# Where the low weights of one kind of unit lie in their slots: a 64-byte shift in a float32 split-matmul kernel

## What is computed

```python
# first block (cut)
zin = rmsnorm(x, gain) @ w_in                       # 2048 x 10240
q, k, v, g_attn, u, g_pool, m_attn, m_pool = split(zin)
y_attn = (stick_breaking_attention(q, k, v) * silu(g_attn)) @ w_attn_up
y_pool = (pooled(u) @ pool_w * pool_scale * silu(g_pool)) @ w_pool_up
x = x + (sigmoid(m_attn) * y_attn + sigmoid(m_pool) * y_pool) @ w_out
# second block (cut)
x = x + hybrid_mixer(rms_norm(x), ...)              # retention and gated delta rule, w_in_2, w_out_2
x = x + cross_attention(rms_norm(x), mem, w_xq_2, w_xkv_2, w_xo_2)
x = x + square(relu(rms_norm(x) @ w_ff1_2)) @ w_ff2_2
return rms_norm(x)
```

## Time and profile before

| | |
|---|---|
| median of three runs | 2882.5 us (2881.85 to 2883.88) |
| time of the profiled execution | 2884.14 us |
| its span, first to last instruction | 2882.4 us |
| TensorE busy | 2847.8 us, 99% |
| VectorE busy | 1931.6 us, 67% |
| ScalarE busy | 1354.6 us, 47% |
| mean DMA rate | 176 GB/s |

### The profile page before, as it was taken

The page is one execution under the profiler, slowest core; times in us unless marked ns, Lnnn a source line. Parts: engine busy times, 40 slices in busy tenths (PEclk is TensorE's granted clock), DMA queues, the critical chain, the costliest instruction groups (busy, mean ns, idle before and its releaser), DMA issues.

```text
span 2882.4 us, 38752 instructions
## 1 busy us (share of the span) xinstructions
PE 2847.8 (99%) x15872; PEld 2443.7 (85%) x15872; DVE 1931.6 (67%) x2513; ACT 1354.6 (47%) x1729; POOL 57.1 (2%) x102
## 2 busy tenths in 40 slices
PE   9999999999999999999999999999999999999998
PEld 8899888888888888888888888888888888888887
DVE  7645557678665658888888875456666555656556
ACT  5434654357443445555554543444345434444434
POOL 0000210000000000000000000000000000000000
PEclk9999999999999999999999999999999999999999
DMA  7544445564555544433333345544354445554453
GB/s 277 183 182 161 146 161 191 189 236 172 196 180 196 198 151 160 147 136 143 144 134 136 140 163 201 193 180 157 133 204 176 188 191 192 190 202 176 187 193 146
DMA packets 72849, 506.66 MB, mean 176 GB/s; under 512 B 8384, under 2 KB 8512, under 8 KB 12896
## 3 DMA queue, kind: packets, MB, share of 16 engines
q1 hardware_dynamic: 71136, 497.83, 46.8%
q0 software_dynamic: 1104, 5.90, 0.6%
q10 hardware_dynamic: 432, 0.45, 0.0%
HBM read 499.95 MB, written 2.10 MB: 174 GB/s over the span
## 4 chain that ended last, share of the span: by engine, by line
PE 86%; DVE 9%; ACT 3%; issue 2%; DMA 1%; SPq 0%; DVEq 0%; POOL 0%; ACTq 0%
PE double L1333 80%; PE bank L1333 5%; DVE cacc L2036 2%; DVE wlo L2030 2%; ACT whi L1692 1%; DVE cst L2053 1%; PE bank L1336 1%; DVE cacc L2033 1%; ACT L1888 0%; DVE Tn L2544 0%; DVE cst L2030 0%; DVE Cm L2030 0%; ACT tmp L1893 0%; DMA vec<-in_vec 0%; DMA raw<-in_wall 0%
## 5 line engine op out<-in xcount | busy, mean ns | idle before, releaser
L1333 PE MATMUL double<-AA,whi 128*128 128x512 f32 (+1 forms) x5008 | 1660.7, 383 | 3.5 <-DVE wlo L2030 3.5
L1333 PE MATMUL double<-AA,wlo 128*128 128x256 f32 (+1 forms) x4624 | 1302.1, 282 | 0.0
L1692 ACT ACTIVATE whi<-raw 128x1024 fp32r<-128x1024 f32 x926 | 925.0, 1049 | 790.1 <-PE double L1333 762.1
L2030 DVE TENSOR_TENSOR wlo<-raw,whi 128x1024 fp32r<-128x1024 f32 (+1 forms) x934 | 1101.4, 1214 | 233.2 <-ACT whi L1692 230.7
L1333 PEld LDWEIGHTS double<-AA,whi 128*128 128x128 f32 x5008 | 916.0, 188 | 197.5 <-DVE wlo L2030 5.1
L1333 PEld LDWEIGHTS double<-AA,wlo 128*128 128x128 f32 x4624 | 871.6, 188 | 1.5
L1333 PE MATMUL double<-whi,AA 128*128 128x512 f32 x1536 | 487.9, 393 | 0.5 <-DVE wlo L2030 0.5
L1333 PEld LDWEIGHTS double<-whi,AA 128*128 128x128 f32 x1536 | 288.4, 188 | 60.9 <-DVE wlo L2030 1.3
L1333 PE MATMUL double<-whi,BB 128*128 128x512 f32 x1024 | 316.9, 389 | 0.0
L1333 PE MATMUL double<-wlo,AA 128*128 128x512 f32 x768 | 299.0, 389 | 0.0
L1333 PEld LDWEIGHTS double<-whi,BB 128*128 128x128 f32 x1024 | 192.2, 188 | 40.3
(11 more groups left out here) (335 smaller groups left out, 1722.6 us busy)
## 6 DMA issues: line engine op xcount, KB each, us to landing
raw<-in_wall SPq DMA_DIRECT2D x462, 1024.0 KB, 4.9
raw<-in_wall SPq DMA_DIRECT2D x9, 256.0 KB, 6.6
X<-in_xT SPq DMA_DIRECT2D x1, 2048.0 KB, 11.4
Mm<-in_memT POOLq DMA_DIRECT2D x1, 2048.0 KB, 16.2
tmp<-rqk POOLq DMA_DIRECT2D x16, 128.0 KB, 2.2
mblk<-in_memT SPq DMA_DIRECT2D x8, 256.0 KB, 4.5
dec<-in_dec POOLq DMA_DIRECT2D x1, 1536.0 KB, 9.3
hs<-in_hsT SPq DMA_DIRECT2D x4, 272.0 KB, 5.5
```

What stands on the lines that cost most here:

```text
L1333: return q.matmul(out, lhsT, rhs, start=start, stop=stop, skip_group_check=True)
L1692: q.activation(whi[j % SPL][:, c], raw[j % RAW][:, c], ACT.Copy).then_inc(S("w_hi"), 1)
L2030: return q.tensor_tensor(out, a, b, o)
```

## The change

The three `wlo` slots get 64 elements more (256 bytes, 8448 instead of 8192 bytes), the three `whi` slots none. In units of kind T the low weights are written and read 16 elements (64 bytes) behind the slot's start; in all other units they stay at the start. The high weights stay where they are in every unit. A line in the arena keeps `AA` at the base's place; it adds nothing here.

```diff
     raw = [ar.get([P_, UNIT], F32, f"raw{i}") for i in range(RAW)]
-    whi = [ar.get([P_, UNIT], F32R, f"whi{i}") for i in range(SPL)]
-    wlo = [ar.get([P_, UNIT], F32R, f"wlo{i}") for i in range(SPL)]
+    whi = [ar.get([P_, UNIT + 0], F32R, f"whi{i}") for i in range(SPL)]
+    wlo = [ar.get([P_, UNIT + 64], F32R, f"wlo{i}") for i in range(SPL)]
+    ar.off += (base - ar.off) % 256
     A_off = ar.off
...
+    def set_off(j):
+        pr = P.pairs[units[j][0]]
+        return (0, 16 if pr["kind"] == "T" else 0)
+
+    def hi_of(j):
+        o = set_off(j)[0]
+        return whi[j % SPL][:, o:o + UNIT]
+
+    def lo_of(j):
+        o = set_off(j)[1]
+        return wlo[j % SPL][:, o:o + UNIT]
...
-            s = j % SPL
-            wh = whi[s][:, 0:kt * nc_].rearrange("p (t c) -> p t c", t=kt)
-            wl = wlo[s][:, 0:kt * nc_].rearrange("p (t c) -> p t c", t=kt)
+            wh = hi_of(j)[:, 0:kt * nc_].rearrange("p (t c) -> p t c", t=kt)
+            wl = lo_of(j)[:, 0:kt * nc_].rearrange("p (t c) -> p t c", t=kt)
...
-            q.activation(whi[j % SPL][:, c], raw[j % RAW][:, c], ACT.Copy).then_inc(S("w_hi"), 1)
+            q.activation(hi_of(j)[:, c], raw[j % RAW][:, c], ACT.Copy).then_inc(S("w_hi"), 1)
...
-            tt(wlo[j % SPL][:, c], raw[j % RAW][:, c], whi[j % SPL][:, c].bitcast(F32), ALU.subtract).then_inc(S("w_lo"), 1)
+            tt(lo_of(j)[:, c], raw[j % RAW][:, c], hi_of(j)[:, c].bitcast(F32), ALU.subtract).then_inc(S("w_lo"), 1)
```

More of the change, by code:

```diff
@@ L1698, in s_hi0 @@
             c = slice(512 * n, 512 * (n + 1))
-            q.activation(whi[j][:, c], raw[j][:, c], ACT.Copy).then_inc(S("w_hi" if n % 2 else "first_hi"), 1)
+            q.activation(hi_of(j)[:, c], raw[j][:, c], ACT.Copy).then_inc(S("w_hi" if n % 2 else "first_hi"), 1)
         def s_load_vec(_, r):
@@ L2065, in s_lo0 @@
             q.wait_ge(S("w_hi" if n % 2 else "first_hi"), 2 * j + n // 2 + 1)
-            tt(wlo[j][:, c], raw[j][:, c], whi[j][:, c].bitcast(F32), ALU.subtract).then_inc(S("w_lo" if n % 2 else "first_lo"), 1)
+            tt(lo_of(j)[:, c], raw[j][:, c], hi_of(j)[:, c].bitcast(F32), ALU.subtract).then_inc(S("w_lo" if n % 2 else "first_lo"), 1)
         def s_a1(k, r):
```

## The result

The changed kernel takes 2868.47 us (median of five runs, 2868.18 to 2870.14), against 2882.5 us before. The ratio is 0.9952, with a 95% interval from 0.9939 to 0.9965. The forecast was 2870.5 us.

A forecast was written before the change was run, and what follows sets the result against it. TensorE's own rate was taken as the bound. From the profiled 2884.1 us, 12.0 us for dear plain units and 0 elsewhere gave 2872.1; the profiled run lying 1.6 above the median, 2870.5 us, range 2857 to 2890.

The forecast's parts named there:

- The bound: Whole kernel: TensorE, busy 2847.8 of 2882.4 us; only its own rate or gated delta rule waits can move the end.
- Plain units outside the gated delta rule: About 112 dear T units drop from 353.3 to 346.6 ns a pair, saving 12.0 us; 36 cheap ones unchanged.
- Rotating units: T units passing through all four distances: mean pair rate stays, 0 us, with 2.2 us to either side.
- Gated delta rule: Its 56 plain T units could gain 6.0 us, but waits grow as much: 0 taken, 3 us kept for range.
- W and N units: Operands keep their places; N stays at 226.6 ns a matmul, no change taken.
- The mechanism: In plain T units the wlo load collides with the high matmul's stream at place 128; moving it 64 bytes ends this.
- The measure of the excess: A T pair's 768 columns need 320 ns at 2.4 GHz, so 27 to 33 ns a pair are extra.
- the supposed bound of 344 ns: Lowest T pair time, taken from unit gab, whose weight loads are a quarter as wide.
- The first: Rival: plain T units land at about 351 ns a pair, nothing measurable, about 2881 us; chance 0.30 with the skill's rule.
- The second: Rival: plain T units lose the cheap state, 354.5 to 357 ns a pair, 2889 to 2895 us; chance 0.22.
- The third: Rival: both loads meet the stream without cost, T pairs near 344 ns, 2858 to 2864 us; chance 0.11.
- The Trainium skill's rule: TensorE's two SBUF read ports are independent, so time stays at 2882.5 us; counted within the first rival's 0.30.

The follow-up runs named there:

- e8: The changed kernel with low weights 64 bytes further in plain T units alone, rotating units' weights at the start: 2868.88 us, ratio to before 0.9956.
- e1: The changed kernel with its pads kept but no unit's low weights shifted: 2882.31 us, ratio to before 1.0001.
- e3: The changed kernel with all weights at their slots' start and activations AA and BB moved by 192 bytes instead: 2894.31 us, ratio to before 1.0041.
- e2: The changed kernel with high weights instead of low ones 64 bytes further in T units: 2864.02 us, ratio to before 0.9939.
- e12: As e2, but units au and wo keep their high weights at the start: 2863.96 us, ratio to before 0.9938.
- e10: As e2, with three more matmuls before each of three entries (wo, fifth mk column block, third xo block): 2865.79 us, ratio to before 0.9947.
- e13: The changed kernel with offsets by group: rotating units high 32 bytes; rq, rk, wo2, f1 high 64; other T units low 64: 2858.66 us, ratio 0.9914.
- e4: The changed kernel with low weights 128 bytes further in T units instead of 64: 2874.64 us, ratio to before 0.9974.
- e5: The changed kernel with low weights 192 bytes further in T units instead of 64: 2875.70 us, ratio to before 0.9976.

## Why the prediction was right, and where its reason was not

**The bound** was read rightly: TensorE's own rate, with the clock at 1.00 throughout. Of the 15.7 us, 13.8 lie in units outside the gated delta rule and the start, where TensorE hardly waits.

**Plain units outside the gated delta rule**: 12.0 us were worked out, 12.3 came. The step from 353.3 to 346.6 ns a pair was exact, and the cheap units kept their rate. The high matmul carries the difference, 399 to 392 ns. The 112 dear and 36 cheap units of the sum are 148 of 168; the other 20 (14 `xq`, 2 `xo`, 4 `f1`) have no term in it. `xq` gained 0.6 us where the sum had 0.2 for two of its units.

**Rotating units**: 0 was taken, 1.5 us came, inside the 2.2 us kept for the range. The reason given for 0, that all distances only change places, says nothing on it: e8 gives `ga` the same 350.0 ns without moving its weights.

**Gated delta rule**: 0 was taken and up to 3 us kept; the stretch got 1.3 us shorter, though the pairs of its plain units that follow one another without a stop got 3.7 us shorter, summed over their starts in the two traces. As forecast, most of it went into waits.

**W and N units**: no change forecast, and N is at 226.7 ns. e1 shows that the 768 bytes are worth at most 0.1%.

**The mechanism** was the weak step. The prediction said that the `wlo` load collides with the stream when both stand at one place, and that moving it breaks the meeting. That a low-weight shift matters and where the excess sits was right. But distance alone does not decide. At the distance of 64 between `wlo` load and stream, e3 has 353.3 ns. At distance 0 the kernel before has 346.6 and 353.3, and e2, whose `wlo` load is at that distance, 340, 350 and 353. What the runs show in its place: in plain stretches the repeated sequence of two loads and two matmuls settles in a repeating pattern with one of a few mean rates (340.0, 346.7, 350.0, 351 to 352, 353.3). Which rates were seen depended on the places of high weights, low weights and activations together. Where several are possible, one is picked when the stage is entered or taken up again after a stop: by the places of what runs ahead (`au` in e12), and also by something that no place explains (`xo` in e1, `dv` in e2, e10 and e12). In the change itself the plain stretches outside the gated delta rule all came out at 346.7; that is what the gain is, the loss of the dear rate. The offsets alone do not ensure it, for `pu` in e13 has them and runs partly at 353.3. The size of the gain was therefore right partly by luck: "the cheap rate that occurs in this kernel" happened to be the rate of the new places, but 350.0 (e4, e5) or 353.3 (e3) would have fitted the stated mechanism as well.

The measure of the excess was off too. The prediction set pairs against 320 ns, which counts one column a cycle at 2.4 GHz; no run shows that rate. By the N units of the earlier trace rows 768 columns take 340 ns, so the excess was 6.7 and 13.3 ns, not 27 to 33, and a rate below the supposed bound of 344 ns could have been expected.

**The rivals.** The first (rates of about 351 at another distance) did not happen here but does at 128 and 192 bytes, with 350.0 ns and a larger gain than it allowed (2874.6 and 2875.7 us, not 2881). The second (the cheap rate lost) did not happen here, but e3 is that case: +0.41%. The third, better than the cheap rate, exists in e2, with a better rate than its bound of 344 ns, and although only one of the two loads was moved there too.

**The Trainium skill's rule**, SBUF — State Buffer, section "Who interferes with whom", says that TensorE's two read ports are independent and that TensorE never waits on anyone. The prediction concluded from it that nothing would change. The runs do not bear that conclusion out: the same instructions take 340 to 353 ns a pair, and the offsets alone move the time by 0.5%. Whether the two ports interfere is not shown by any row.

What stays open: why the rates are these, and whether a stage such as `xo` keeps its rate from one execution of a kernel to the next. No row of a trace shows a read or a collision, so that reads collide at all is argued, not shown. Shifting both loads of a unit with the activations at place 128 was not tried, and neither were shifts between 32 and 64 bytes.

## What to carry to other kernels

When TensorE is busy all the time, divide stretches of equal work by their matmuls and compare them: two rates for one shape are time to be had, and here moving one operand by 32 or 64 bytes within its 256 was worth 0.5%, and offsets by group 0.9%. Measure each offset, with the stages ahead of it in place; a rate read from another stage, or from another distance, did not carry over (128 bytes, both loads apart). An offset at which all stages came out at one rate is the safer choice, but look again when the offsets of the stages ahead change: `pu` in e13 ran partly at 353.3 with other offsets around it. And take more than one trace before a rate is called a stage's own.

## What the runs showed of the hardware

- The same pair of matmuls (512 and 256 float32r columns, with a 128-column weight load each) took 340.0 to 353.3 ns in plain stretches, at a granted clock of 1.00, by the addresses of its operands modulo 256 and by how the stretch was entered.
- 340.0 ns for 768 columns (`wo2` in e2) is 0.443 ns a column, the same as 226.7 ns for 512 in the N units. No plain stretch was faster.
- At the same addresses and behind the same work, the first unit of `dv` ran at 353.1, 340.0 and 350.0 ns a pair in e2, e10 and e12.
- A stage that runs without a stop keeps its pattern: `wo2` does through its 16 units, 256 pairs but for the first ones, in every trace. The seven `f1` blocks behind an `f2` block have one rate in the kernel before and in e1, 353.2 ns each.
- A shift of 32 bytes of the low weights already does what 64 do (2868.30 and 2868.47 us), while for the high weights 32 and 64 bytes differ by 11 ns a pair in `wo2` (351.1 and 340.1).
- N units took 226.7 ns a matmul in all kernels but one; with the activations at place 64 they took 228.9.
